# First block's attention: VectorE's side work split around the division of probabilities, branch tiles between the last weighing, flip and weighing

## The reference

```
for l in range(2):                                    # first block
    x = x + 0.5 * swiglu(rms_norm(x), ...)
    z = rms_norm(x) @ w_in                            # q_a k_a v_a, q_b f_b i_b, og_b, gate_a gate_b
    y_a = dilated_attention(rope(q_a), rope(k_a), v_a) @ w_att_branch     # 4 heads, 3 groups
    o_b = hgrn2_recurrence(q_b, f_b, i_b)
    o_b = rms_norm(o_b, head_norm) * silu(og_b)
    y_b = o_b @ w_hgrn_branch
    merged = sigmoid(gate_a) * y_a + sigmoid(gate_b) * y_b
    x = x + merged @ w_mix_out
    x = x + cross_attention(...); x = x + 0.5 * swiglu(...)
# second block: two layers of another kind; not touched
```

## Time and profile before

| | us |
|---|---|
| median of 3 runs | 3028.66 |
| lowest, highest | 3024.89, 3028.89 |
| profiled execution, its own time | 3025.48 |
| its span (first to last instruction) | 3023.4 |
| PE busy | 2936.3 (97%) |
| DVE busy | 2093.2 (69%) |
| ACT busy | 1312.0 (43%) |

### The profile page before, as it was taken

How to read it: one execution, slowest core, us unless ns; L and a number is a source line. 1 busy time by engine, 2 the same in 40 slices (tenths; PEclk the granted TensorE clock), 3 DMA queues, 4 the chain that set the end, 5 groups by cost and what they waited for, 6 DMA issues and landing times.

```text
span 3023.4 us, 52341 instructions
## 1 busy us (share of the span) xinstructions
PE 2936.3 (97%) x23186; PEld 2863.7 (95%) x23196; DVE 2093.2 (69%) x2644; ACT 1312.0 (43%) x1300; POOL 210.9 (7%) x163
## 2 busy tenths in 40 slices
PE   9999999999999999999999999999899999998999
PEld 8999999999999999998999999998699999986999
DVE  7777866556677677867556677677676766776644
ACT  5334545454334335545444334344543333445432
POOL 0000420000000000510000000003000000030000
PEclk9999999999999999999999999999899999998999
DMA  7654333445666645433445665644156666541354
GB/s 270 241 211 167 140 140 126 155 152 182 252 226 223 240 185 178 147 119 132 168 148 203 243 223 208 239 182 141 55 192 241 224 222 237 183 145 49 142 186 147
DMA packets 78464, 549.07 MB, mean 182 GB/s; under 512 B 8480, under 2 KB 11936, under 8 KB 12320
## 3 DMA queue, kind: packets, MB, share of 16 engines
q1 hardware_dynamic: 67152, 464.99, 43.1%
q0 software_dynamic: 11088, 80.75, 6.8%
HBM read 544.65 MB, written 1.05 MB: 180 GB/s over the span
## 4 chain that ended last, share of the span: by engine, by line
PE 79%; DVE 13%; ACT 4%; POOL 2%; issue 2%; DMA 0%; DVEq 0%; POOLq 0%; SPq 0%; ACTq 0%
PE ps L301 71%; DVE ring_lo L295 4%; ACT w_hi L288 2%; PE ps L373 1%; POOL qk L1492 1%; PE ps L497 1%; DVE hk L1201 1%; PE ps L747 1%; POOL rope_a L1488 1%; DVE e L378 0%; PE ps L877 0%; DVE e L1259 0%; DVE a_hg L1279 0%; DVE e L1258 0%; PE ps L1587 0%
## 5 line engine op out<-in xcount | busy, mean ns | idle before, releaser
L295 DVE TENSOR_TENSOR ring_lo<-ring,w_hi 128x2048 fp32r<-128x2048 f32 x438 | 1009.9, 2308 | 639.4 <-ACT w_hi L288 634.8
L301 PE MATMUL ps<-h_hi,w_hi 128*128 128x256 f32 x4688 | 1348.0, 288 | 21.8 <-DVE h_lo L410 8.9
L301 PE MATMUL ps<-h_lo,w_hi 128*128 128x256 f32 x4688 | 1333.9, 285 | 0.0
L301 PE MATMUL ps<-h_hi,ring_lo 128*128 128x256 f32 x4688 | 1333.4, 284 | 0.0
L288 ACT ACTIVATE w_hi<-ring 128x2048 fp32r<-128x2048 f32 x438 | 836.3, 1910 | 726.6 <-PE ps L301 626.4
L301 PEld LDWEIGHTS ps<-h_hi,w_hi 128*128 128x128 f32 x4688 | 907.8, 194 | 31.5 <-issue 23.3
L301 PEld LDWEIGHTS ps<-h_lo,w_hi 128*128 128x128 f32 x4688 | 908.0, 194 | 3.2 <-issue 2.4
L301 PEld LDWEIGHTS ps<-h_hi,ring_lo 128*128 128x128 f32 x4688 | 907.3, 194 | 0.0
L301 PE MATMUL ps<-g_hi,w_hi 128*128 128x256 f32 x1408 | 398.5, 283 | 0.0
L301 PE MATMUL ps<-g_lo,w_hi 128*128 128x256 f32 x1408 | 398.5, 283 | 0.0
L301 PE MATMUL ps<-g_hi,ring_lo 128*128 128x256 f32 x1408 | 398.5, 283 | 0.0
(11 more groups left out here) (309 smaller groups left out, 3138.1 us busy)
## 6 DMA issues: line engine op xcount, KB each, us to landing
ring<-stream SPq DMA_DIRECT2D x438, 1024.0 KB, 4.8
e<-ada POOLq DMA_DIRECT2D x77, 1024.0 KB, 5.2
x<-x_t SPq DMA_DIRECT2D x4, 256.0 KB, 4.4
mem<-mem_t SPq DMA_DIRECT2D x1, 1024.0 KB, 9.1
out_t<-x SPq DMA_DIRECT2D x4, 256.0 KB, 2.1
con_sb<-con SPq DMA_DIRECT2D x1, 896.0 KB, 14.8
con_sb<-con SPq DMA_DIRECT2D x1, 640.0 KB, 5.9
hq<-lmask SPq DMA_DIRECT2D x1, 512.0 KB, 15.6
```

Of the source, the lines that this page charges most:

```text
L295: nc.vector.tensor_tensor(ring_lo[:, p % RING, :], ring[:, p % RING, :], w_hi[:, p % HIGHS, :].bitcast(F32), ALU.subtract).then_inc(S.w_lo ...
L301: mm = nc.tensor.matmul(out, a, b, start=start and n == 0, stop=stop and n == 2, skip_group_check=group)
```

## The change

Three engines' code is written in another order; no instruction is added or dropped.

- DVE: `o_gated`, `o_scaled` and `o_split` are each cut in two parts. The first part (four of eight products; one of four operations; the cast) stays between `soften` and `normalise`. The second follows later: of head 0 between its two `low`, of heads 1 and 2 after both `low`. The first `low` after `normalise` now stands ahead of `att_low(h-1)`. For head 3, `low` of branch tiles 2 and 3 follow `att_low(2)` and stand ahead of `att_low(3)`.
- PE: flip of head 3 moves from ahead of branch tile 0 to behind it, and weigh of head 3 from ahead of branch tile 1 to behind it.
- ACT: `high` of branch tile 3 moves ahead of `flipped(3)`, and `high` of branch tile 4 (that is M_YA) ahead of `weighed(3)`.

```diff
@@ one_pe
                 if hd < 3:
                     gate_tile(n)
                     n += 1
-                flip(hd)
+                    flip(hd)
 
             pe.wait_ge(S.scores_read, nth(S.scores_read, 2 * HEADS))
             pe.wait_ge(S.o_ready, nth(S.o_ready, 1))
             project(pe, M_YB, 4, (o_hi, o_lo))
+            flip(HEADS - 1)
+            project(pe, M_YB + 1, 5, (o_hi, o_lo))
             weigh(HEADS - 1)
-            for b in (1, 2):
-                project(pe, M_YB + b, 4 + b, (o_hi, o_lo))
+            project(pe, M_YB + 2, 6, (o_hi, o_lo))
             pe.wait_ge(S.att_ready, nth(S.att_ready, HEADS))
             project(pe, M_YB + 3, 7, (o_hi, o_lo))
@@ one_act
                 if hd < 3:
                     gate(n)
                     n += 1
-                flipped(hd)
+                    flipped(hd)
+
+            act.wait_ge(S.tile_done, M_YB + 1)
+            high(act, M_YB + HIGHS)
+            flipped(HEADS - 1)
+            act.wait_ge(S.tile_done, M_YB + 2)
+            high(act, M_YB + 1 + HIGHS)
             weighed(HEADS - 1)
...
-            for b in range(4):
+            for b in (2, 3):
                 act.wait_ge(S.tile_done, M_YB + b + 1)
                 high(act, M_YB + b + HIGHS)
@@ one_dve
-            def o_gated():
-                dve.wait_ge(S.evac_done, nth(S.evac_done, 34))
-                for hd in range(HG):
+            def o_gated(part):
+                if part == 0:
+                    dve.wait_ge(S.evac_done, nth(S.evac_done, 34))
+                for hd in range(4 * part, 4 * part + 4):
...
-                chain(ins)
+                if part == 1:
+                    chain(ins)
 
-            def o_scaled():
-                dve.wait_ge(S.o_rstd, nth(S.o_rstd, 1))
-                refine(chain, hi_flat, hq_flat)
+            def o_scaled(part):
+                if part == 0:
+                    dve.wait_ge(S.o_rstd, nth(S.o_rstd, 1))
+                    chain(nc.vector.scalar_tensor_tensor(out=hq_flat, in0=hi_flat, scalar=-0.5, in1=hq_flat,
+                                                         op0=ALU.mult, op1=ALU.mult))
+                    return
+                chain(nc.vector.tensor_tensor(hq_flat, hq_flat, hi_flat, ALU.mult))
+                chain(nc.vector.scalar_tensor_tensor(out=hi_flat, in0=hq_flat, scalar=1.5, in1=hi_flat,
+                                                     op0=ALU.add, op1=ALU.mult))
                 chain(nc.vector.tensor_tensor(hk_flat, hk_flat, hi_flat, ALU.mult))
 
-            def o_split():
-                chain(nc.vector.tensor_copy(o_hi[:], hk[:]))
+            def o_split(part):
+                if part == 0:
+                    chain(nc.vector.tensor_copy(o_hi[:], hk[:]))
+                    return
                 nc.vector.tensor_tensor(o_lo[:], hk[:], o_hi[:].bitcast(F32), ALU.subtract).then_inc(S.o_ready, 1)
...
                 soften(hd, parts, hd, C(C_M1, 9 * P), DH ** -0.5, 0)
                 if hd < 3:
-                    (o_gated, o_scaled, o_split)[hd]()
+                    (o_gated, o_scaled, o_split)[hd](0)
                 normalise(hd, hd, 0, ((0, 3 * P), (3 * P, 9 * P)))
+                if hd < 3:
+                    low(dve, M_OG + 5 + 2 * hd + HIGHS)
+                if hd == 0:
+                    o_gated(1)
                 if hd >= 1:
                     att_low(hd - 1)
-                low(dve, M_OG + 5 + 2 * hd + HIGHS)
                 if hd < 3:
                     low(dve, M_OG + 6 + 2 * hd + HIGHS)
+                if hd in (1, 2):
+                    (o_scaled, o_split)[hd - 1](1)
+            low(dve, M_YB - 1 + HIGHS)
+            low(dve, M_YB + HIGHS)
             att_low(HEADS - 1)
...
-                low(dve, M_YB + b + HIGHS)
+                if b >= 1:
+                    low(dve, M_YB + b + HIGHS)
```

## The result

| | us |
|---|---|
| changed kernel, median of 16 runs | 3034.13 (3030.75 to 3035.90) |
| kernel before, median of 16 runs beside them | 3028.31 (3024.89 to 3031.07) |
| ratio, 95% interval | 1.0019 (1.0012 to 1.0026) |
| profiled execution of the changed kernel: own time, span | 3030.98, 3029.0 |

The change costs 5.8 us at the medians, 3.6 to 7.9 by the interval. The forecast was 3031.0, in a range of 3025 to 3036.5, and "within 0.2%" as the likeliest case. 0.19% is just inside that bound, though the interval shows that it is a loss.

What follows compares the result with a forecast made beforehand. PE, busy 97% of the span, was taken as the bound. Two layers of 0.1 us of moved waits plus 1.6 of low clock gave +3.4 us: 3028.9 on the profiled execution, 3032.1 on the median; 3031.0 was taken, range 3025 to 3036.5.

Steps and rivals of the forecast that it cites:

- within 0.2%: Whole program: a measured time not distinguishable from no change, about 6 us either way; chance 0.74.
- The moved waits: PE's flips, per layer: gains of 1.46, 1.2 and 1.9 us at flips 0, 1 and 3, loss of 4.6 at flip 2.
- sum without the clock: One layer's attention stage: waits won and lost plus 0.1 us for the change of steps, together +0.1 us.
- DVE's at 526.75: Trace row where DVE stood 4.82 us on a ring_lo with head 3's softening behind it; cited for first-in, first-out queues.
- Head 3: PE's flip 3 behind branch tile 0: no wait, gain 1.90 us a layer, with 4.4 us in hand.
- Behind the stage: After weigh 3: later mem_lo, two gating products and M_YA's ring_lo stay hidden, with 0.9 us in hand; no cost.
- The clock: PE behind flip 2: the wait of 4.6 us brings a fall to half clock, costing 1.6 us a layer, ends 0 and 3.4.
- rival C: Behind flip 2: 6.8 us of low clock in each layer, or a wait 1.5 us longer; +7.0 us, 3032.5 to 3035.7; chance 0.20.
- four short falls of five: Earlier trace: PE's five waits of 3.8 to 4.3 us each brought a clock fall, four of them short.
- A: The forecast itself: wait at flip 2 and a short clock fall; +3.4 us, 3029 to 3032; chance 0.58.
- B: Flip 2 waits without a clock fall, or with one mostly inside the wait; +0.2 us, 3025.7 to 3028.9; chance 0.15.
- D: Softening 2 isn't held up and flip 2 doesn't wait; -9.1 us, 3016.4 to 3019.6; chance 0.07.

Runs made afterwards that it cites:

- e3: Changed kernel plus 36 dummy matmuls on PE between gate tile 10 and flip 2; ratio to the kernel before 0.9998.
- e2: Kernel before with only the PE and ACT part, head 3's flip and weigh moved later, DVE's side work whole; ratio to the kernel before 0.9976.
- e6: Changed kernel with head 3's flip, ACT's order and the end of DVE's order put back; 3033.3 us, ratio to the kernel before 1.0020.
- e1: Changed kernel with att_lo again ahead of the first ring_lo after the division; ratio to the kernel before 0.9998.
- e7: Kernel before with head 3's flip and weigh moved later and only head 0's four products split off; 3031.2 us, ratio to the kernel before 1.0013.
- e4: Changed kernel with head 1's four large operations together again between softening 1 and division 1; 3033.9 us, ratio to the kernel before 1.0021.
- e5: Changed kernel with side work placed where DVE stands idle and att_lo ahead of both ring_lo; 3019.97 us, ratio to the kernel before 0.9969.
- e2b: Repeat on another chip of the kernel before with only head 3's flip and weigh moved later; ratio to the kernel before 0.9977.
- e9: Kernel before with head 3's flip and weigh moved later, plus 15 dummy matmuls ahead of flip 2; 3027.01 us against 3026.74 for the kernel before.
- e8: Changed kernel plus 18 dummy matmuls on PE between gate tile 10 and flip 2; ratio to the kernel before 1.0004.

## Why the prediction was right or wrong

**The moved waits: right.** Each time of the forecast, beside the trace of the first layer:

| | forecast | measured |
|---|---|---|
| flip 0 | 488.2 | 488.38 |
| softening 1 | 495.35 | 495.58 |
| flip 1 | 505.0 | 505.20 |
| second `ring_lo` of head 1, done | 509.5 | 509.68 |
| softening 2 | 516.5 | 516.65 |
| `att_lo` of head 1's weighing, start | 525.5 | 525.71 |
| flip 2 | 526.05 | 526.27 |
| bracket at flip 2 | 4.4 | 4.48 |
| flip 3 | 542.5 and the clock | 544.38 |
| M_YA | 562.7 and the clock | 564.59 |

The times run 0.2 us late from the start: ACT's exponentials of head 0 began at 485.52, 0.18 later than in the earlier trace rows. The forecast's sum without the clock was +0.1 us a layer; e3, where the clock is kept up, measures +0.3 and +0.1. It could be exact because ACT and DVE did nothing out of program order in these rows: the next event is the later of two sums.

The row that the prediction gave for this order, DVE's at 526.75, does not test it. PE's scores of head 3 ran from 525.11 to about 527 there, so softening 3 had nothing to work on while DVE stood. The changed kernel's `ring_lo` at 507.47 does: DVE stood 2.42 us for ACT, with L1341 behind it, whose operands were written by the operation that ended at 500.6.

**Head 3: right.** From flip 2 to flip 3 it is 18.11 us (526.27 to 544.38): 10.61 + 5.83, and 1.67 for the clock. Flip 3 does not wait. e2 shows the part alone, 1.6 to 1.9 us a layer for the 1.90 forecast.

**Behind the stage: right.** `mem_lo` began at 556.88 and M_YA's `ring_lo` was out at 563.54, 1.05 us ahead of 564.59; 0.9 was forecast.

**The clock: right in kind, too small in size.** This is the step that missed, the term of 1.6 us a layer. Measured by the changed kernel's stage less e3's, it is 1.66 in the first layer and 2.76 in the second. The second is rival C's fall of 6.8 us, of which 1.2 us lie inside the wait: half of the other 5.6 is 2.8. I had taken four short falls of five as the odds. The changed kernel and the experiments give ten falls at waits ahead of a flip. The loss is the time from this flip until PE is ready for the next, less the 16.44 us of full speed (for e6 10.61):

| bracket at the flip | fall in the first, second layer | loss behind the flip |
|---|---|---|
| 2.92 (e1) | 3.4, 3.4 | 1.67, 1.67 |
| 4.28 (e7) | 6.8, 3.4 | 2.80, 1.66 |
| 4.48 (changed) | 3.4, 6.8 | 1.67, 2.76 |
| 4.48, 4.47 (e6) | 6.8, 6.8 | 2.66, 2.15 |
| 6.48 (e4) | 6.8, 6.8 | 1.80, 1.65 |

The longer wait has the longer fall more often, but not the larger loss: in e4 3.1 and 3.4 us of the fall pass while PE stands anyway. Each loss is half of the low clock that lies behind the flip, within 0.1 us. For a wait of 4.5 us the mean of the four is 2.3 us, between A and C, where the forecast had 1.6. So what the term had wrong is how often the fall is long: the forecast took one in five, and it was six of these ten, three of four at a wait of 4.5 us. Its price of 1.7 for a short fall wholly behind the wait is what all four short ones cost. Against the forecast change of 3.4 us the stage gives 4.9, and the time 5.8; the last 0.9 is within the interval. The rest of the miss on 3031.0 is the base: the prediction started from 3027.6, and the runs beside the changed kernel gave 3028.3.

**The rivals.** B (no fall) is refuted by the windows, and e3 shows what it would have been worth. D (flip 2 not waiting) is refuted by the bracket; its gain exists, but needs e5's order. C's fall held in one layer of two, and the time, 3034.1, lies above A's own range (3028 to 3033) and inside C's (3032.5 to 3035.7). That the change stayed under 0.2% as forecast was close: 0.19%, where the forecast's own term was 0.11%.

## What to carry to other kernels

When work is moved off one step of a chain that repeats, follow it to the next round: e7 and e4 show that the wait moves to the following flip, larger, unless the work lands where its engine stood idle, as in e5. A sum of waits that comes out at zero is still a loss if it turns three short waits into one long one, since in this stage the clock fell at the long ones only; here that cost 1.7 to 2.8 us each, half of the low clock behind the wait. An independent part of a change (here flip 3) is worth timing alone: by the stage it was a gain of 3.5 us inside a change that lost 5.

## What the runs showed of the hardware

- TensorE's clock did not fall at flips that had waited 1.33 to 2.32 us (before, e2, e2b, e9, flip 3 of e6, e8), in any layer of any trace, but fell in all ten cases from 2.92 to 6.48. Elsewhere in the program, a wait of 1.09 us was followed by a fall and the same wait in another execution was not. The length of the wait alone doesn't decide.
- The ten falls in the stage last 3.4 us or 6.8, none anything between.
- A fall cost half of its part behind the wait: 1.65 us for 6.8 us of low clock of which 3.4 lay in a wait of 6.48 (e4, second layer), 2.80 for 6.8 us of which 1.0 lay in a wait of 4.28 (e7, first layer).
- 36 matmuls of no use, in a wait of 4.5 us, gave back 1.66 and 2.76 us of the stage; 18 did as well by the stage (1.79 and 2.75), though the time of that kernel fell less.
